# Couples 3 and 4 of the up projection by seven products, with two factors of h2 made on GpSimd

## The reference

```
h2 = rmsnorm(x, norm_pre2) * (1 + sc2[:, None]) + sh2[:, None]
a, gt = jnp.split(h2 @ w_up, 2, axis=-1)          # (T, 1024) @ (1024, 2 * 2816)
a_conv, ffn_buf_new = causal_dwconv(a, ffn_buf, ffn_conv_w, ffn_conv_b)   # 3 taps
f = (jax.nn.gelu(a_conv) * gt) @ w_down
x = x + g2[:, None] * rmsnorm(f, norm_post2)
```

## Time and profile before

| | |
|---|---|
| median of 3 runs | 984.46 us (982.47 to 985.14) |
| the profiled execution | 982.37 us, its span 980.6 us |
| TensorE matmul busy | 965.4 us, 7623 matmuls |
| VectorE busy | 559.5 us |
| ScalarE busy | 424.5 us |
| GpSimd busy | 219.9 us |
| TensorE's granted clock over the span | 1.00 |

### The profile page before, as it was taken

One profiled execution on the slowest core, in us unless ns is written; L12 is line 12 of the kernel. 1 busy time (PEld: TensorE's weight loads), 2 busy tenths in 40 slices (PEclk: granted clock), 3 DMA queues, 4 the chain that ended last, 5 costly groups with the idle time before them and its releaser, 6 DMA issues.

```text
span 980.6 us, 18504 instructions
## 1 busy us (share of the span) xinstructions
PE 965.4 (98%) x7623; PEld 877.5 (89%) x7623; DVE 559.5 (57%) x842; ACT 424.5 (43%) x668; POOL 219.9 (22%) x121
## 2 busy tenths in 40 slices
PE   6999999999999999999999999999999999999997
PEld 4889889999999999899898889999999999888886
DVE  2511106485665564346438588878999988660204
ACT  4545323234433333443454355345565556633212
POOL 3043533243343343233344000000000000013430
PEclk9999999999999999999999999999999999999999
DMA  9675343797465758545437032223333332422312
GB/s 332 230 118 172 119 75 92 155 95 150 155 162 145 147 130 135 94 114 151 121 106 225 1 114 69 77 65 101 95 87 96 99 97 75 122 73 86 87 52 96
DMA packets 145028, 115.58 MB, mean 118 GB/s; under 512 B 11225, under 2 KB 121585, under 8 KB 144945
## 3 DMA queue, kind: packets, MB, share of 16 engines
q1 hardware_dynamic: 144849, 114.38, 46.5%
q10 hardware_dynamic: 96, 0.04, 0.0%
HBM read 107.02 MB, written 7.35 MB: 117 GB/s over the span
## 4 chain that ended last, share of the span: by engine, by line
PE 96%; ACT 1%; DVE 1%; DMA 1%; issue 0%; SPq 0%; DVEq 0%; ACTq 0%
PE pair L2154 41%; PE pair L2571 19%; PE pair L2260 17%; PE pair L2528 5%; PE pair L2144 2%; PE pair L2341 1%; PE pair L2314 1%; PE pair L2084 1%; DMA x_tok<-in_x_prompt 1%; PE pair L2252 1%; PE pair L2404 1%; PE pair L2393 1%; PE pair L2253 1%; PE pair L2254 1%; PE pair L2251 1%; PE pair L2448 1%
## 5 line engine op out<-in xcount | busy, mean ns | idle before, releaser
L931 POOL TENSOR_TENSOR w_lo<-raw,w_hi 128x1024 fp32r<-128x1024 f32 x53 | 129.2, 2439 | 539.1 <-ACT w_hi L1005 539.1
L2154 PE MATMUL pair<-h_hi,w_hi 128*128 128x288 f32 x1008 | 227.4, 302 | 0.1
L2154 PE MATMUL pair<-h_hi,w_lo 128*128 128x288 f32 x1008 | 220.9, 296 | 0.0
L2154 PE MATMUL pair<-h_lo,w_hi 128*128 128x288 f32 x1008 | 220.6, 295 | 0.0
L2154 PEld LDWEIGHTS pair<-h_hi,w_hi 128*128 128x128 f32 x1008 | 163.5, 189 | 18.4 <-issue 15.9
L2154 PEld LDWEIGHTS pair<-h_hi,w_lo 128*128 128x128 f32 x1008 | 163.8, 188 | 0.0
L2154 PEld LDWEIGHTS pair<-h_lo,w_hi 128*128 128x128 f32 x1008 | 163.8, 188 | 0.0
L1005 ACT ACTIVATE w_hi<-raw 128x1024 fp32r<-128x1024 f32 x66 | 69.6, 1057 | 163.2 <-PE pair L2254 80.2
L931 POOL TENSOR_TENSOR w_lo<-raw_c,w_hi 128x1024 fp32r<-128x1024 f32 x24 | 67.6, 2818 | 126.7 <-ACT w_hi L1005 126.7
L2571 PE MATMUL pair<-t_hi,w_hi 128*128 128x288 f32 x272 | 80.5, 296 | 0.3 <-ACT u_buf L1280 0.3
L2571 PE MATMUL pair<-t_lo,w_hi 128*128 128x288 f32 x272 | 80.3, 295 | 0.0
(11 more groups left out here) (368 smaller groups left out, 1725.9 us busy)
## 6 DMA issues: line engine op xcount, KB each, us to landing
raw_c<-in_w_ada SPq DMA_DIRECT2D x32, 512.0 KB, 5.5
raw<-in_w_in SPq DMA_DIRECT2D x224, 64.0 KB, 3.3
raw_c<-in_w_in SPq DMA_DIRECT2D x192, 64.0 KB, 3.6
raw<-in_w_up SPq DMA_DIRECT2D x24, 512.0 KB, 3.8
raw<-in_w_down SPq DMA_DIRECT2D x22, 512.0 KB, 3.7
raw_up<-in_w_up SPq DMA_DIRECT2D x20, 512.0 KB, 3.8
ada_first<-in_w_ada SPq DMA_DIRECT2D x16, 512.0 KB, 10.0
raw<-in_w_in SPq DMA_DIRECT2D x8, 512.0 KB, 4.6
```

The costliest lines, as they stand in the source:

```text
L931: pool.tensor_tensor(lo, raw_tile(n)[:, :], hi.bitcast(F32), ALU.subtract).then_inc(S("w_lo_done"), 1)
L2154: ins = pe.matmul(bank[pair][:, half, 0:HALF], w[:, i, :], x[:, i, HALF * half:HALF * half + HALF], start=i == 0 and p == 0, stop=i == KT ...
```

## The change

`FIRST_SEVEN` becomes 3. The factors `t_32[2]` and `t_32[3]` are made by GpSimd after `t_32[1]`. VectorE's row up to couple 3 is rewritten: the factors' low parts come in two pairs, after the convolutions of couples 0 and 1. ScalarE's row has slots a to d of couple 3 where the high parts of couples 3 and 4 stood. TensorE waits for the factors' low parts one by one.

```
-FIRST_SEVEN = 5
+FIRST_SEVEN = 3
...
                     low(n, hi[:, :], lo[:, :], n + 1)
+            pool.wait_ge(S("s_add"), 3)
+            b12, b21, b22 = h2_all[:, 0:4, HALF:T], h2_all[:, 4:8, 0:HALF], h2_all[:, 4:8, HALF:T]
+            pool.tensor_tensor(t_32[2][:, :, :], b22, b12, ALU.subtract).then_inc(S("s_add"), 1)
+            pool.tensor_tensor(t_32[3][:, :, :], b21, t_32[1][:, :, :], ALU.subtract).then_inc(S("s_add"), 1)
             pool.wait_ge(S("w_lo_done"), TILE_DN + 9)
...
             gelu(0)
             evict(1)
-            for x in range(2):
-                up_high(3, x)
+            a_high(FIRST_SEVEN)
+            b_high(FIRST_SEVEN)
             gelu(1)
             evict(2)
-            gelu(2)
-            for x in range(2):
-                up_high(4, x)
-            evict(3)
-            gelu(3)
-            a_high(FIRST_SEVEN)
-            b_high(FIRST_SEVEN)
-            evict(4)
             c_high(FIRST_SEVEN)
             d_high(FIRST_SEVEN)
...
             up_lows(2)
-            dve.tensor_tensor(t_32[2][:, :, :], b22, b12, ALU.subtract).then_inc(S("s_add"), 1)
-            dve.wait_ge(S("s_add"), 3)
-            dve.tensor_tensor(t_32[3][:, :, :], b21, t_32[1][:, :, :], ALU.subtract).then_inc(S("s_add"), 1)
-            whole_pair(0)
-            up_lows(3)
-            whole_pair(1)
-            for i in range(4):
+
+            def factor_low(i):
                 dve.wait_ge(S("h2_hi_done"), TT + i + 1)
...
-            whole_pair(2)
-            up_lows(4)
...
-            whole_pair(3)
+            history(0)
+            convolve(0)
+            factor_low(0)
+            factor_low(1)
+            gate(0)
             sums12(FIRST_SEVEN)
             a_low(FIRST_SEVEN)
+            history(1)
+            convolve(1)
+            factor_low(2)
+            factor_low(3)
+            gate(1)
             b_low(FIRST_SEVEN)
-            history(4)
-            convolve(4)
             sums34(FIRST_SEVEN)
+            history(2)
+            convolve(2)
             c_low(FIRST_SEVEN)
-            gate(4)
+            gate(2)
...
+                def factors_made(n):
+                    if s == 0:
+                        pe.wait_ge(S("h2_lo_done"), TT + n)
+
                 pe.wait_ge(S("w_lo_done"), LOW_AT["a", j])
                 if s < 2:
-                    pe.wait_ge(S("a_done"), 3 * 4)
+                    pe.wait_ge(S("a_done"), 3 * (FIRST_SEVEN - 1))
...
                 if s == 0:
-                    pe.wait_ge(S("f_done"), 3 * 4)
+                    pe.wait_ge(S("f_done"), 3 * (FIRST_SEVEN - 1))
...
                 pe.wait_ge(S("a_done"), 3 * j + 1)
+                factors_made(2)
                 product(slot_b, 1, t2, x, False)
```

More of the change, by code:

```diff
@@ L2548, in whole_tiles @@
                         (hi, lo), pair = (slot_d if x else slot_a), x
-                        last = max(i for i in range(j) if not seven(i) and (i > 4 or i % 2 == 0))
+                        last = max(i for i in range(j) if not seven(i) and (i >= FIRST_SEVEN or i % 2 == 0))
                     if x == 0:
@@ L2594, in seven_products @@
                 pe.wait_ge(S("a_done"), 3 * j + 2)
+                factors_made(3)
                 product(slot_c, 0, t3, x, False)
@@ L2599, in seven_products @@
                 pe.wait_ge(S("c_sum"), 4 * s + 2)
+                factors_made(4)
                 product(slot_d, 0, t4, x, False)
@@ L2621, in _ @@
                 if seven(j):
-                    if j == FIRST_SEVEN:
-                        pe.wait_ge(S("h2_lo_done"), TT + 4)
                     seven_products(j)
```

## The result

| | median | range | ratio to before, 95% interval |
|---|---|---|---|
| before | 983.11 us | 982.05 to 985.14 (13 runs) | |
| after | 985.73 us | 984.56 to 987.14 (13 runs) | 1.0025 [1.0018, 1.0033] |
| profiled execution of after | 987.14 us, span 985.4 | | |

What follows compares the result with a forecast made beforehand. TensorE, busy 965.4 of 980.6 us, was taken as the bound. Removed matmuls -3.2 us plus four stalls +5.4 us gave +2.2 us, 986.7 us as a median; range -2.2 us (982.3) to +3.9 us (988.4).

Steps and rivals of the forecast that it cites:

- The removed work: TensorE, couples 3 and 4: 12 matmuls fewer each, 24 x 132.8 ns, 3.19 us saved.
- The two factors on GpSimd: Around couple 2, engines take whole instructions in turn: VectorE gains 5.3 us where 2.54 us were taken away.
- the engines don't meet: Rival: GpSimd lets VectorE run on; -1.8 us, 982.7 us, chance 0.13, plus 0.05 for no stall, -3.2 us.
- the dear turn: Rival: GpSimd's instruction lasts 3.27 us, VectorE loses 6.5 us; kernel +3.4 us, 987.9 us, chance 0.22.
- the rival of +0.0: Only VectorE's history copy and first tap are held by GpSimd; time unchanged, 984.5 us, chance 0.10.
- VectorE's row: VectorE up to couple 3: gate 0 at 613.2 us, gate 1 at 621.65; TensorE stalls 2.0 and 0.5 us.
- ScalarE's queue: Couple 3: first product's copy stands behind slots c and d, done at 626.1 us; TensorE's third product waits 2.8 us.
- The fourth wait: TensorE's seventh product of couple 3 waits 0.1 us for VectorE's c22.
- The granted clock I leave at full: Clock stays 1.00 despite stalls, as in the first 100 us with TensorE idle 9.4 us in pieces; no cost.
- TensorE's restart: Within the rival of dearer turns: whatever TensorE loses restarting after a stall pushes the time up too; no size given.
- nothing past it waited: From couple 4, starting at 634.2 us instead of 628.8, VectorE's lag is within what is allowed; no further stall.

Runs made afterwards that it cites:

- e6: e5 with history, first tap and tails of couples 0 to 2 on ScalarE, and sums ahead of gates: 979.65 us, ratio 0.9974.
- e2: The kernel before, couples 3 and 4 whole, with only the third and fourth factor moved to GpSimd: 983.18 us, ratio 1.0003.
- e1: The changed kernel with the third and fourth factor back on VectorE: 983.61 us, ratio 1.0007.
- e7: e6 with the third and fourth factor on GpSimd instead of VectorE: 982.94 us, ratio 1.0000.
- e3: The changed kernel with ScalarE's copies of couple 3's first and third product ahead of slots c and d: 985.19 us, ratio 1.0019.
- e5: The changed kernel with both e1's and e3's edits: 982.59 us, ratio 1.0001.
- e4: The changed kernel with 16 unused transposes on TensorE in the wait before couple 3's third product: 985.21 us, ratio 1.0026; again 984.99 us, 1.0021.

## Why the forecast held, step by step

**The removed work**, -3.19 us: right. e6, with the waits gone, has a stretch 3.31 us shorter than before's, the same within the 0.65 us that e2 shows.

**The two factors on GpSimd: right in mechanism, a little dear.** I had GpSimd's instructions end at 603.35 and 607.15 us; in before's time (after's less the 1.53) they end at 603.29 and 606.92. The forecast took 5.3 us added to VectorE; the rows give (4.83 - 2.55) + (2.65 - 0.17) = 4.8. e1 against after gives 2.2 us of the stretch, e7 against e6 2.24, where the forecast's terms gave 2.8 (5.3 less 2.54) and the rows' own give 2.2 (4.76 less 2.54). The rival that the engines don't meet is excluded by the rows and by e1; so is the dear turn of 3.27 us. The SBUF page of the Trainium skill ("Who interferes with whom") calls this contention an exclusive lock, and has a VectorE instruction with two SBUF inputs contend with a GpSimd instruction that reads SBUF; the trace agrees, with the 4.83 us. The narrower rule of the Trainium skill's Advanced Engine Details and Errata ("VectorE Performance Modes"), from which the rival of +0.0 came, would have left the second 128x1024 subtraction at 1.2 us. It took some 3.6 (4.83 less 1.2), in after and e2 alike.

**VectorE's row**: gate 0 done at 612.78 us (forecast 613.2), gate 1 at 621.22 (621.65): 0.4 us early. Its waits cost 1.9 and 0.4 us from start to start (drawn as 1.9 and 0.2) instead of 2.0 and 0.5. The forecast's own times, 613.15 less 611.27 us, give 1.9 for the first as well.

**ScalarE's queue**: slot c started at 623.67 (624.2), `u_buf` was done at 625.55 (626.1), and the wait cost 2.6 us from start to start (drawn as 2.4) instead of 2.8. The size was right, but the step reads as though the order cost 2.8 us by itself, and e3 and e5 show that it does not. With the order turned round, the same 2.3 us are waited for VectorE's low parts. The fourth wait of 0.1 us for `c22` did not come.

**"The granted clock I leave at full": this step failed.** I drew it from the first 100 us, with 9.4 us of idle time in pieces, but took no note of what the pieces were. The two longest, and the same 128x128 transposes behind them and later, in before:

```profile
PE pair L2050 <- DMA rows_c<-in_c_sample: 7.0, 1, 7.0
PE pair L2079 <- DVE c_wide L1449: 1.1, 1, 1.1
```

```profile
8.38 4.95 PE L2079 MATMUL pair<-ident 128*128 128x128 f32 x22 [1.07 <-DVE c_wide L1449]
...
24.60 1.91 PE L2079 MATMUL pair<-ident 128*128 128x128 f32 x16
```

7.0 of the 9.4 us stand ahead of TensorE's first instruction at 6.95 us, and no pause behind it is longer than 1.1 us. So these rows say nothing of a pause of 2.4 us. Nor do they show full pace at the start: 0.23 us a transpose from 8.38 us on and 0.12 later, though the clock is given as 1.00 for both; why is open. In the changed kernel one pause of 2.4 us, with one of 1.9 us that ended ten microseconds before it, was followed by the level of 1.2 GHz in all three profiles, at 1.6 us, and by the mean clocks probably in 18 of 23 executions. The pauses of 1.7 to 1.9 us were not so followed in any profile of after, e3 or e4. The forecast named TensorE's restart only in a rival, without a price.

So two errors offset each other in part, and some of the agreement is luck: waits of 4.9 us in place of 5.4, and 1.6 us of clock that I did not count. By the waits alone the change is worth +1.7 us (e4's two profiles: +1.8), with the clock +3.2 us in a profile, and the median of the first, mixed executions, +2.6, lies between. The repeats, all with the mean clock of 0.997, lie at +3.8 us by the medians. The 0.6 us above the stretch are open: in their profiles the stretch also begins later, at 597.35 and 597.74 us against 595.41 in before, behind work that the change does not touch. Couple 4 started at 636.75 - 1.53 = 635.2 us instead of 634.2, by the clock's 1.6 less 0.5 of shorter waits, and nothing past it waited that does not wait in before, as forecast.

## What to carry to other kernels

Before work is given to GpSimd, look at what VectorE does in that moment: if it reads two operands from SBUF, or copies within it, as it did here, VectorE pays for the whole of GpSimd's instruction (2.2 us lost at the end for 2.5 us taken off it), and ScalarE was the engine that had room (e6). Where a wait ends is not what it waits for: e3 moved TensorE's wait to another releaser without shortening it, so the engine whose row is full must be found and shortened. And a pause of the bounding engine is priced with what follows it: list the longest single pauses, not their sum, and read the granted clock behind each.

## What I had not expected of the hardware

- Behind a pause of 2.4 us the granted clock went to 0.50 (1.2 GHz) for 628 to 631 us, and 36 matmuls took 6.37 us instead of 4.78. All four profiles with such a pause show the fall (after three times, e1); by the mean clock it came in some 18 of 23 executions of after. Filling the pause with 16 transposes (1.91 us), or splitting it in two of 1.2 us at most, kept it at 1.00 in the profile.
- A tiny instruction is held for as long as a large one: a VectorE copy of 128x16, 0.17 us by itself, took 2.65, as a subtraction of 128x1152 took 3.83 instead of 1.35 (e7), 2.5 us more in both.
- Two profiles with the same work in a stretch of 56 us can differ by 0.65 us (before and e2), by 131.1 against 133.3 ns a matmul, while repeats of one kernel differ by 0.02 (59.23, 59.24, 59.25). What makes one program's pace differ from another's is open.
